# Recurrence of a hybrid encoder layer: the two score levels of a round are issued apart, the second behind the product with the turned inverse

## The chip, the cores and the metric

The kernel runs on one core of one Trainium2 chip. The metric is the device time of one execution in microseconds. TensorE is called PE here (with PEld for its weight loads), VectorE is DVE, ScalarE is ACT, SyncE is SP.

## What is computed

One step of a one-layer encoder trunk over 2048 prompt tokens and 8 short streams of 16 tokens: an adaptive norm, a projection, two parallel groups of recurrent heads (four HGRN2 heads of 128, eight RWKV-7 heads of 64), an output projection, then a two-level mixture of experts and a final norm. The change touches the recurrence alone. Its two parts are, in the reference:

```python
def step(S, blk):                       # HGRN2, by chunks of 64 tokens
    ...
    scores = jnp.einsum('bhtd,bhsd,bhtsd->bhts', qc, kc, decay)
    o = (jnp.einsum('bhts,bhsv->bhtv', scores, vc)
         + jnp.einsum('bhtd,bhdv->bhtv', qc * jnp.exp(b), S))
...
def step(S, inp):                       # RWKV-7, token by token
    sa = jnp.einsum('bhij,bhj->bhi', S, -kk_t)
    S = (S * jnp.exp(lw_t)[:, :, None, :] + sa[..., None] * (kk_t * a_t)[:, :, None, :]
         + v_t[..., None] * k_t[:, :, None, :])
    y = jnp.einsum('bhij,bhj->bhi', S, r_t)
```

## The kernel before

The program is a row of stages, one after the other: projections (to about 1,240 us), the recurrence (1,240 to about 1,930 us), the merge with the output projection, the experts. Each stage writes one instruction stream for each engine by hand. An engine works through its stream in the order written; `wait_ge` holds it until a counting semaphore has reached a value, and `then_inc` on an instruction raises one.

The recurrence (`recur`) takes 17 fronts of 128 tokens, each two chunks of 64. Step `i` of the loop handles the state-free work of front `f = i` and the state-bound work of the front before it (`b = i - 1`). One pass of this loop is called a step here, numbered by `f`: 0 has no back part, 1 to 15 are full, 16 (`TAIL`) holds the eight short streams and has four levels in place of six.

The state-free work has two parts that share PE:

- The inverse of a unit triangular 64 x 64 matrix for each of 8 heads and 2 chunks, built in doubling levels `lv`. A level is `make_y` (L1160, product of `LB` and `X` into `P_Y`), `turn_x` (L1168, the transpose of `X`, by a product with the identity, into `P_XT`) and `make_x` (L1180, the product with the turned inverse `XT`, added into `P_X`). Between them DVE masks `P_Y` into `Y` (`mask_y`, L1562, or L1560 at the first and last level), ACT copies `P_XT` to `XT` (`keep_xt`, L1417) and `P_X` to `X` (`keep_x`, L1411). So `make_x(lv)` waits for `mask_y(lv)` and `keep_xt(lv - 1)`, and `make_y(lv + 1)` waits for `keep_x(lv)`. The last level has `make_xt` (L1193) in place of `make_x`.
- The attention scores of the HGRN2 heads, for levels `n = 0` to 6: 8 products each (4 heads, 2 chunks, L1212) into one half of the bank `P_S`, even `n` left and odd `n` right. DVE writes them to `att` under the mask of the level (`mask_score`, L1573 and L1576, 128 x 256 elements each). `P_S` holds two levels, called a round `r = n // 2` in the code; the first level of a round waits until DVE has taken both of the round before (`scored`). DVE takes a round when `score_made` has been raised, once a round, with its last product.

Each full-precision product shows as two records in the trace, so 8 products are x16 and 16 products x32.

The order written on PE is, for levels 2 to 5: `make_y(lv)`, `turn_x(lv - 1)`, `score(lv - 1)`, `make_x(lv)`. The order on DVE, which the change leaves as it is:

```python
for lv in range(2, levels(f)):
    mask_y(f, lv)
    if back and lv == 2:
        y_centre(b)
    mask_score(f, lv - 1)
    if back and lv == 3:
        y_variance(b)
        y_bonus(b)
```

`y_centre`, `y_variance` (L1616, L1618) and `y_bonus` (L1625, L1627) are parts of the group norm of front `b`. ACT at level 2 has `keep_xt(1)`, then the square of the centred `y` (L1447, waits for `y_centre`), then `keep_x(2)`; at level 3 `keep_xt(2)`, `keep_x(3)`, then a logarithm and an exponential that wait for `y_variance`.

Of the kernel before, what the change touches and what calls it, by code (L numbers as in the profile page):

```python
# [43 lines left out]
HK_B, HK_KD, HK_Q, HK_K = [N_LEVELS + n for n in range(4)]  # L44
# [34 lines left out]
def sem_of(nc, names, name):  # L79

    names.append(nc.alloc_semaphore(name))
    return names[-1]
# [767 lines left out]
def recur(nc, t, bonus, ends):  # L850

    names = []
    with ExitStack() as ctx:
# [5 lines left out]
        def ev(name):  # L859

            if name not in sems:
                sems[name] = sem_of(nc, names, "re_" + name)
            return sems[name]
# [7 lines left out]
        hkf = [sb(f"hkf{p}", [128, 4, N_HK, 128]) for p in range(2)]  # L871
# [41 lines left out]
        P_X, P_Y, P_XT, P_S, P_ST, P_O = [ctx.enter_context(nc.psum_tensor(f"re_P{b}", [128, 512], F32)) for b in range(6)]  # L913
# [5 lines left out]
        def chunk(c):  # L919
            return slice(CH * c, CH * c + CH)  # L920
# [25 lines left out]
        def levels(f):  # L946
            return N_LEVELS if f < TAIL else DEC.bit_length() - 1
# [77 lines left out]
        def _(eng):  # L1025
# [145 lines left out]
            def make_x(f, lv):  # L1171

                for g in range(2):
                    eng.wait_ge(ev("y_kept"), before(f, 10) + 2 * (lv - 1) + g + 1)
                    if lv > 1:
                        eng.wait_ge(ev("xt_kept"), before(f, 8) + 2 * (lv - 2) + g + 1)
                    left, right = (XT0, Y1) if lv == 1 else (XT, Y)
                    for h in range(4 * g, 4 * g + 4):
                        for c in range(2):
                            ins = eng.matmul(P_X[chunk(c), 64 * h:64 * h + 64], left[chunk(c), h, :], right[chunk(c), h, :],  # L1180
                                             start=(lv == 1 and h == 0), stop=(h % 4 == 3), skip_group_check=True)
                ins.then_inc(ev("x_made"), 1)

            def make_xt(f):

                lv = levels(f) - 1
                left = Y5 if lv == 5 else Y3
                eng.wait_ge(ev("xt_kept"), before(f, 8) + 2 * (lv - 2) + 2)
                for g in range(2):
                    eng.wait_ge(ev("y_kept"), before(f, 10) + 2 * (lv - 1) + g + 1)  # L1190
                    for h in range(4 * g, 4 * g + 4):
                        for c in range(2):
                            ins = eng.matmul(P_XT[chunk(c), 64 * h:64 * h + 64], left[chunk(c), h, :], XT[chunk(c), h, :],  # L1193
                                             start=(h == 0), stop=(h % 4 == 3), skip_group_check=True)
                ins.then_inc(ev("xtf_made"), 1)


            def score(f, r):

                if 2 * r > levels(f):  # L1200
                    return
                p = f % 2
                if r == 0:
                    eng.wait_ge(ev("x0_kept"), f + 1)
                else:
                    eng.wait_ge(ev("scored"), before(f, 7) + 2 * r)
                for n in range(2 * r, min(2 * r + 2, levels(f) + 1)):
                    a, b = (HK_K, HK_Q) if n == 0 else (n - 1, n - 1)
                    for h in range(4):
                        o = 256 * (n % 2) + 64 * h  # L1210
                        for c in range(2):
                            ins = eng.matmul(P_S[chunk(c), o:o + 64], hkf[p][:, h, a, chunk(c)], hkf[p][:, h, b, chunk(c)],  # L1212
                                             start=(n % 2 == 0 and h == 0), stop=(h == 3), skip_group_check=True)
                ins.then_inc(ev("score_made"), 1)

            def turn_kd(f):

# [22 lines left out]
            for i in range(TAIL + 1):  # L1240
                f, b = i, i - 1
                p = f % 2
                back = b >= 0
                if back:
                    h_update(b)
                    h_inter(b, 0)
                    from_state(b, 0)
                    from_values(b, 0)
                eng.wait_ge(ev(f"front_in{p}"), 128 * (f // 2 + 1) + (64 if f == TAIL else 0))
                if f:  # L1250
                    eng.wait_ge(ev("x_kept"), before(f, 8))
                turn(f, RK_V, P_X)
                if f:
                    eng.wait_ge(ev("y_kept"), before(f, 10))
                turn(f, RK_B0, P_Y)
                if back:
                    solve(b, 0)
                    eng.wait_ge(ev("s_kept"), 2 * f)
                turn(f, RK_B1, P_XT)
                eng.wait_ge(ev("tok_kept"), 3 * f + 1)  # L1260
                products(f, RK_B0, (P_S, P_X))
                if back:
                    to_state(b, 0)
                    y_from_state(b, 0)
                eng.wait_ge(ev("tok_kept"), 3 * f + 3)
                products(f, RK_B1, (P_Y, P_XT))
                if back:
                    h_inter(b, 1)
                    h_intra(b)
                turn_x0(f)  # L1270
                if back:
                    from_state(b, 1)
                    from_values(b, 1)
                make_y(f, 1)
                if back:
                    solve(b, 1)
                make_x(f, 1)
                if back:
                    to_state(b, 1)
                    y_from_state(b, 1)  # L1280
                score(f, 0)
                if back:
                    y_out(b)
                for lv in range(2, levels(f)):
                    make_y(f, lv)
                    turn_x(f, lv - 1)
                    score(f, lv - 1)
                    if lv < levels(f) - 1:
                        make_x(f, lv)
                    else:  # L1290
                        make_xt(f)
                turn_kd(f)
                from_tokens(f)


            p = TAIL % 2
# [7 lines left out]
            for q in range(4):  # L1304
                if q >= 2:
                    eng.wait_ge(ev("std_begun"), q - 1)
                for m in range(4):
                    ins = eng.transpose((P_X, P_Y)[q % 2][:, 128 * m:128 * m + 128], srow[:, q, 128 * m:128 * m + 128], ident)
# [3 lines left out]
            for m in range(4):  # L1312
                ins = eng.transpose(P_XT[0:RW_N, 128 * m:128 * m + 128], ST[:, m, :], ident)
# [4 lines left out]
            for h in range(4):  # L1318
                o = slice(128 * h, 128 * h + 128)
                for c in range(2):  # L1320
                    eng.matmul(out_o(chunk(c), h), att[p][chunk(c), h, :], tmb[p][chunk(c), 0, o], start=(h == 0), stop=False, skip_group_check=True)
            for n in range(2):
                for h in range(4):
                    for g in range(4):
                        ins = eng.matmul(out_o(quarter(g), h), qbd[n][:, h, quarter(g)], Sd[:, 2 * g + n, h, :], start=False, stop=(n == 1 and h == 3),
                                         skip_group_check=True)
# [3 lines left out]
            for n in range(2):  # L1330
                for h in range(8):
                    for g in range(4):
                        ins = eng.matmul(out_g(quarter(g), h), ard[n][half(h), h // 2, 0, quarter(g)], STd[half(h), g, h // 2, n, :],
                                         start=False, stop=(n == 1 and h == 7), skip_group_check=True)
# [3 lines left out]
            for n in range(2):  # L1338
                for h in range(4):
                    o = slice(128 * h, 128 * h + 128)  # L1340
                    for g in range(4):
                        if n and h == 0:
                            eng.wait_ge(ev("sd_kept"), g + 1)
                        ins = eng.matmul(banks[g][:, o], kdT[p][quarter(g), o], hd[n][quarter(g), o], start=(h == 0), stop=(h == 3), skip_group_check=True)
                ins.then_inc(ev("upd_made"), 1)
                if n == 0:
                    eng.wait_ge(ev("g_kept"), 2 * TAIL + 1)
                    for h in range(8):
                        for c in range(2):
                            ins = eng.matmul(out_g(chunk(c), h), XTF[p][chunk(c), h, :], G[chunk(c), 64 * h:64 * h + 64],  # L1350
                                             start=False, stop=(h == 7), skip_group_check=True)
                    ins.then_inc(ev("sa_made"), 1)
            eng.wait_ge(ev("sad_kept"), 1)
            for n in range(2):
                for h in range(8):
                    for g in range(4):
                        ins = eng.matmul(out_y(quarter(g), h), ard[n][half(h), h // 2, 1, quarter(g)], STd[half(h), g, h // 2, n, :],
                                         start=False, stop=False, skip_group_check=True)
            ins.then_inc(ev("ys_made"), 1)
            eng.wait_ge(ev("ys_made"), 2 * TAIL + 1)  # L1360
            for h in range(8):
                for c in range(2):
                    ins = eng.matmul(out_y(chunk(c), h), LB[p][chunk(c), h, 1, :], SA[chunk(c), 64 * h:64 * h + 64],
                                     start=False, stop=(h == 7), skip_group_check=True)
            ins.then_inc(ev("yo_made"), 1)
            for g in range(4):
                eng.wait_ge(ev("sd_kept"), 5 + g)
                for kind, right in ((2, vd), (1, SAd)):
                    for n in range(2):
                        for h in range(8):  # L1370
                            o = slice(256 * n + 64 * (h // 2), 256 * n + 64 * (h // 2) + 64)
                            ins = eng.matmul(banks[g][half(h), o], tok[p][quarter(g), kind, 64 * h:64 * h + 64], right[n][quarter(g), 64 * h:64 * h + 64],
                                             start=(kind == 2 and n == 0 and h < 2), stop=(kind == 1 and n == 1 and h >= 6), skip_group_check=True)
                ins.then_inc(ev("std_made"), 1)
            for q in range(4):
                eng.wait_ge(ev("std_kept"), q + 1)
                for m in range(4):
                    ins = eng.transpose(banks[q][:, 128 * m:128 * m + 128], STd[:, q, m, :, :].rearrange("p s v -> p (s v)"), ident)
# [1163 lines left out]
```

## Time and profile before

| | |
|---|---|
| median of 3 runs | 3448.4 us (3444.95 to 3451.6) |
| the profiled execution: time, span | 3456.8 us, 3455.0 us |
| granted TensorE clock, mean of the span | 0.939 of full speed |
| PE busy over the span | 2997.6 us (87%) |
| DVE, ACT busy over the span | 1368.5 us (40%), 982.8 us (28%) |

The profiled execution is a single one, 8.4 us above the median of the runs. Times of single instructions are read from it; in the timeline the first column is the start in us from the span's start, the second the time from the first start to the last end of the merged rows, and the bracket is the idle time of that engine before it, with what ended it.

### The profile page before, as it was taken

The numbers are of one execution on the slowest core, as the hardware profiler recorded it, in microseconds if no ns is written. First come the engines' busy times: TensorE is split into PE (matmuls) and PEld (weight loads), VectorE is DVE, ScalarE is ACT, GpSimd is POOL, SyncE is SP. The second block draws the span as 40 slices with busy tenths as digits, with TensorE's granted clock in tenths as the row PEclk, the third lists the DMA queues.
The fourth block names the chain that finished last, engine by engine and source line by source line (L and its number), as shares of the span: only waits on it lengthen the run. The fifth ranks groups of instructions, "written<-read, shape, count | busy, mean of one in ns | idle before, by whom it ended". The sixth has DMA issues, their size and how long they took to land. (4 is left out here: it accounts for less than half of the span.)

```text
span 3455.0 us, 67244 instructions
## 1 busy us (share of the span) xinstructions
PE 2997.6 (87%) x28271; PEld 1796.4 (52%) x28272; DVE 1368.5 (40%) x3251; ACT 982.8 (28%) x1762; POOL 184.9 (5%) x281
## 2 busy tenths in 40 slices
PE   3899998998989659999999589958999999999930
PEld 1344444444444358888888445535555555555510
DVE  2410156455555535555555334452222112121246
ACT  2421244444434413323323111211222122222223
POOL 0000000000000000000000000000101001010024
PEclk7999999999999879999999799979999999999965
DMA  6233224122232295556553453355886568686746
GB/s 237 78 98 133 103 97 138 52 104 101 90 133 85 102 238 143 143 149 172 163 157 92 142 178 121 122 165 182 294 321 241 193 240 311 225 297 216 262 155 219
DMA packets 373004, 577.74 MB, mean 167 GB/s; under 512 B 31490, under 2 KB 199482, under 8 KB 369728
## 3 DMA queue, kind: packets, MB, share of 16 engines
q1 hardware_dynamic: 337632, 467.22, 40.4%
q0 software_dynamic: 18080, 72.10, 6.3%
q10 hardware_dynamic: 17088, 35.40, 3.3%
q8 instruction: 164, 2.69, 0.3%
q14 instruction: 40, 0.33, 0.0%
HBM read 429.04 MB, written 145.62 MB: 166 GB/s over the span
## 5 line engine op out<-in xcount | busy, mean ns | idle before, releaser
L2309 PE MATMUL moe_PG<-wgu,moe_xT 128*64 128x256 f32 x5248 | 582.1, 380 | 0.7 <-ACT moe_xT L2241 0.7
L441 PE MATMUL pj_P<-pj_hT,pj_wc 128*128 128x512 f32 x1280 | 561.0, 594 | 3.6 <-ACT pj_stage L559 3.6
L2309 PEld LDWEIGHTS moe_PG<-wgu,moe_xT 128*64 128x64 f32 x5248 | 377.3, 137 | 226.2 <-issue 47.5
L441 PEld LDWEIGHTS pj_P<-pj_hT,pj_wc 128*128 128x128 f32 x1280 | 240.9, 190 | 304.5 <-issue 304.5
L2316 PE MATMUL moe_PY<-wd,moe_hT 128*64 128x512 f32 x1312 | 317.7, 603 | 0.0
L1879 PE MATMUL merge_PO<-merge_w,merge_mT 128*128 128x512 f32 x544 | 243.9, 607 | 2.2 <-DMA merge_w<-in_w_out 2.2
L2244 ACT ACT_TABLE_LOAD x82 | 105.2, 1283 | 491.1 <-issue 491.0
L1879 PEld LDWEIGHTS merge_PO<-merge_w,merge_mT 128*128 128x128 f32 x544 | 104.4, 195 | 128.6 <-issue 128.6
L2224 DVE TENSOR_TENSOR moe_sg<-moe_sg,moe_PG 128x128 f32<-128x128 f32 x164 | 46.3, 282 | 290.8 <-ACT moe_sg L2244 290.8
L2228 DVE COPY moe_hT<-moe_PH 128x128 f32<-128x128 f32 x164 | 47.8, 291 | 273.1 <-PE moe_PH L2301 273.1
L2316 PEld LDWEIGHTS moe_PY<-wd,moe_hT 128*64 128x64 f32 x1312 | 81.9, 136 | 120.2 <-issue 86.8
L2231 DVE COPY moe_y<-moe_PY 128x512 f32<-128x512 f32 x82 | 56.7, 691 | 208.3 <-PE moe_PY L2316 208.3
L2263 POOL COPY moe_row<-moe_rows 128x1 int32 x83 | 15.2, 183 | 2126.1 <-issue 1336.9
L1160 PE MATMUL re_P<-re_X,re_LB 64*64 64x64 f32 x2656 | 96.7, 220 | 25.8 <-ACT re_X L1411 23.0
L362 PE MATMUL pj_P<-pj_wt,pj_hT 128*128 128x512 f32 x256 | 114.6, 601 | 1.2 <-ACT pj_hT L518 1.2
L473 PE MATMUL pj_P<-pj_wt,pj_hT 128*128 128x512 f32 x256 | 114.1, 599 | 0.0
L386 PE MATMUL pj_P<-pj_hT,pj_hk 128*128 128x512 f32 x256 | 111.4, 593 | 0.0
L1160 PEld LDWEIGHTS re_P<-re_X,re_LB 64*64 64x64 f32 x2656 | 85.4, 135 | 33.5 <-ACT re_X L1411 29.7
L1417 ACT COPY re_XT<-re_P 128x256 f32<-128x256 f32 x132 | 42.7, 375 | 168.7 <-PE re_P L1168 168.7
L2246 ACT ACTIVATE moe_sg<-moe_PG 128x128 f32<-128x128 f32 x82 | 22.8, 278 | 226.3 <-PE moe_PG L2309 226.3
L2266 POOL DMA_INDIRECT moe_xg<-scratch_h,moe_row x83 | 80.9, 975 | 67.2 <-POOL moe_row L2263 67.2
L791 DVE SCALAR_TENSOR_TENSOR pj_lf<-pj_P,pj_z 128x512 f32<-128x512 f32 (+1 forms) x20 | 12.2, 612 | 181.3 <-ACT pj_z L623 181.3
(373 smaller groups left out, 4222.8 us busy)
## 6 DMA issues: line engine op xcount, KB each, us to landing
wgu<-in_w_gate SPq DMA_DIRECT2D x32, 2048.0 KB, 9.3
wgu<-in_w_up SPq DMA_DIRECT2D x32, 2048.0 KB, 14.9
wd<-in_w_down SPq DMA_DIRECT2D x32, 2048.0 KB, 16.6
re_hkf<-scratch_hk SPq DMA_DIRECT2D x64, 640.0 KB, 8.3
scratch_hk<-pj_hk SPq DMA_DIRECT2D x16, 1536.0 KB, 5.6
re_rkf<-scratch_rk SPq DMA_DIRECT2D x68, 320.0 KB, 4.9
scratch_y_rows<-moe_y ACTq DMA_DIRECT2D x164, 128.0 KB, 5.0
scratch_rk<-pj_rk SPq DMA_DIRECT2D x16, 1280.0 KB, 4.8
```

What stands on the lines that cost most here:

```text
L362: ins = eng.matmul(P[2 + m % 2][:, :], rows[:, k, :], wt[:, k, :], start=(k == 0), stop=(k == KD - 1))
L386: ins = eng.matmul(out, lora_w[:, k, c0:c0 + 128], rhs, start=(s == 0 and k == 0), stop=(s == 1 and k == KD - 1))
L441: ins = eng.matmul(bank[:, :], wc[:, j, k, :], hT[:, k, token(g) + 1:token(g) + 513], start=(k == 0), stop=(k == KD - 1))
L473: ins = eng.matmul(PQ[:, :], rows[:, k, :], wt[:, k, :], start=(k == 0), stop=(k == KD - 1))
L1160: ins = eng.matmul(P_Y[chunk(c), 64 * h:64 * h + 64], LB[f % 2][chunk(c), h, 0, :], X[chunk(c), h, :], start=(h == 0), stop=(h % 4 == 3), ...
L1879: ins = eng.matmul(PO[:, half, :], mT[:, n % 2, k, :], w[:, k, 512 * half:512 * half + 512], start=(k == 0), stop=(k == KD - 1))
L2228: eng.tensor_copy(hT[:, j, :], PH[:, j, 0:128]).then_inc(ev("hT_kept"), 1)
L2231: eng.tensor_copy(y[:, :], PY[:, :]).then_inc(ev("y_kept"), 1)
L2244: eng.activation(sg[:, 0, :], PG[:, 0, 0:128], ACT.Sigmoid).then_inc(ev("sigmoid_made"), 1)
L2266: eng.indirect_dma_start(xg[:, :], None, t["h2"].rearrange("t (h c) -> (t h) c", h=2), bass.IndirectOffsetOnAxis(ap=row[:, 0:1], axis=0)). ...
L2309: ins = eng.matmul(PG[64 * c:64 * c + 64, j, 0:256].rearrange("p (a b) -> p a b", a=2), x_rows, wgu[p][:, :, k, o:o + 128], start=(k == 0) ...
L2316: ins = eng.matmul(PY[64 * n:64 * n + 64, :], hT[:, j, 64 * c:64 * c + 64], wd[p][:, 2 * c + j, 512 * n:512 * n + 512], start=(j == 0 and ...
```

## The change

`score(f, n)` now issues one level `n` in place of a round of two. Before the level loop both levels of round 0 are issued together, as before. In the loop the even level `2 * lv - 2` stays where the pair was, and the odd level `2 * lv - 1` comes behind `make_x(lv)`; at the last level, where `make_xt` is, both stay ahead of it. The wait for `scored` stays with the even level and `score_made` is raised with the odd one (or with the last level there is), so the counts do not change, and DVE and ACT are not touched. With six levels the calls that issue something are 2 and 3 at `lv = 2`, 4 and 5 at `lv = 3`, and 6 alone at `lv = 4`. With four levels (step 16) they are 2 and 3, and 4 alone.

```diff
-            def score(f, r):
-
-                if 2 * r > levels(f):
+            def score(f, n):
+
+                if n > levels(f):
                     return
-                p = f % 2
-                if r == 0:
+                p, r = f % 2, n // 2
+                if n == 0:
                     eng.wait_ge(ev("x0_kept"), f + 1)
-                else:
+                elif n % 2 == 0:
                     eng.wait_ge(ev("scored"), before(f, 7) + 2 * r)
-                for n in range(2 * r, min(2 * r + 2, levels(f) + 1)):
-                    a, b = (HK_K, HK_Q) if n == 0 else (n - 1, n - 1)
-                    for h in range(4):
...
+                a, b = (HK_K, HK_Q) if n == 0 else (n - 1, n - 1)
+                for h in range(4):
...
-                ins.then_inc(ev("score_made"), 1)
+                if n % 2 or n == levels(f):
+                    ins.then_inc(ev("score_made"), 1)
...
                 score(f, 0)
+                score(f, 1)
...
                     turn_x(f, lv - 1)
-                    score(f, lv - 1)
+                    score(f, 2 * lv - 2)
                     if lv < levels(f) - 1:
                         make_x(f, lv)
+                        score(f, 2 * lv - 1)
                     else:
+                        score(f, 2 * lv - 1)
                         make_xt(f)
```

## Rows read from the trace of the kernel before

**Rows 1.** The page: span and number of instructions.
```profile
span 3455.0 us, 67244 instructions
```

**Rows 2.** Busy time by engine, 590 us of the recurrence: length, then PE, PEld, DVE, ACT, POOL.
```profile
1270.00:1860.00 590.00, 547.98 (x14528) 508.53 (x14528) 337.43 (x773) 181.73 (x459) 0.00 (x0) 0.99 0.55 154
```

**Rows 3.** Waits, 1270 to 1860 us: total us, times, longest us.
```profile
ACT re_X L1411 <- PE re_P L1180: 48.6, 50, 2.3
...
DVE re_Y L1562 <- PE re_P L1160: 24.9, 16, 2.6
...
PE re_P L1160 <- ACT re_X L1411: 20.6, 44, 0.5
```

**Rows 4.** Timeline, step 9, level 2 and the start of level 3.
```profile
1612.96 1.01 PEld L1212 LDWEIGHTS re_P<-re_hkf 128*64 128x64 f32 x32
...
1614.04 1.01 PEld L1180 LDWEIGHTS re_P<-re_Y,re_XT 64*64 64x64 f32 x32
...
1614.64 0.63 ACT L1447 ACTIVATE re_ysq<-re_yc 128x512 f32<-128x512 f32 x1 [0.91 <-DVE re_yc L1611]
1615.24 0.65 ACT L1411 COPY re_X<-re_P 128x256 f32<-128x256 f32 x2
1615.66 1.01 PEld L1160 LDWEIGHTS re_P<-re_X,re_LB 64*64 64x64 f32 x32 [0.61 <-ACT re_X L1411]
```

**Rows 5.** Timeline, step 9, level 3 and the start of level 4.
```profile
1616.59 1.02 PEld L1168 LDWEIGHTS re_P<-re_const,re_X 64*64 64x64 f32 x32
...
1616.86 0.76 DVE L1562 TENSOR_TENSOR re_Y<-re_P,re_const 128x256 f32<-128x256 f32 x2 [1.43 <-PE re_P L1160]
1617.67 1.01 PEld L1212 LDWEIGHTS re_P<-re_hkf 128*64 128x64 f32 x32
...
1617.79 0.65 ACT L1417 COPY re_XT<-re_P 128x256 f32<-128x256 f32 x2 [1.91 <-PE re_P L1168]
1618.76 1.01 PEld L1180 LDWEIGHTS re_P<-re_Y,re_XT 64*64 64x64 f32 x32
...
1618.88 0.92 DVE L1576 COPY_PREDICATED re_att<-re_const,re_P 128x256 f32<-128x256 uint32 x2 [1.26 <-PE re_P L1212]
...
1619.95 0.65 ACT L1411 COPY re_X<-re_P 128x256 f32<-128x256 f32 x2 [1.51 <-PE re_P L1180]
1620.38 1.01 PEld L1160 LDWEIGHTS re_P<-re_X,re_LB 64*64 64x64 f32 x32 [0.61 <-ACT re_X L1411]
```

**Rows 6.** Timeline, step 9, level 4.
```profile
1621.20 0.69 DVE L1627 TENSOR_TENSOR re_vb<-re_vb,re_rows 128x512 f32<-128x512 f32 x1
...
1621.81 0.75 DVE L1562 TENSOR_TENSOR re_Y<-re_P,re_const 128x256 f32<-128x256 f32 x2
1622.39 0.55 PEld L1212 LDWEIGHTS re_P<-re_hkf 128*64 128x64 f32 x16
...
1623.00 1.03 PEld L1180 LDWEIGHTS re_P<-re_Y,re_XT 64*64 64x64 f32 x32
...
1623.12 0.45 DVE L1576 COPY_PREDICATED re_att<-re_const,re_P 128x256 f32<-128x256 uint32 x1 [0.57 <-PE re_P L1212]
```

**Rows 7.** Timeline, step 9, earlier: first mask of `Y1`, then the first `make_x`.
```profile
1606.24 0.78 DVE L1560 COPY_PREDICATED re_Y<-re_const,re_P 128x256 f32<-128x256 uint32 x2 [1.27 <-PE re_P L1160]
...
1606.75 0.19 PEld L1180 LDWEIGHTS re_P<-re_Y,re_XT 64*64 64x64 f32 x2
```

**Rows 8.** Timeline, ACT at level 2 of step 1, and the row of all these squares.
```profile
1297.68 0.63 ACT L1447 ACTIVATE re_ysq<-re_yc 128x512 f32<-128x512 f32 x1 [0.91 <-DVE re_yc L1611]
1298.28 0.65 ACT L1411 COPY re_X<-re_P 128x256 f32<-128x256 f32 x2
...
L1447 ACT ACTIVATE re_ysq<-re_yc x15: 630/630/644, 1297.7 to 1852.4; 128x512 f32<-128x512 f32 x15
```

**Rows 9.** Timeline, level 2 of step 10: `turn_x` resumed, then ACT.
```profile
1653.17 0.56 PE L1168 MATMUL re_P<-re_const,re_X 64*64 64x64 f32 x12 [1.42 <-issue]
...
1654.30 0.64 ACT L1447 ACTIVATE re_ysq<-re_yc 128x512 f32<-128x512 f32 x1
...
1655.94 0.65 ACT L1411 COPY re_X<-re_P 128x256 f32<-128x256 f32 x2 [0.99 <-PE re_P L1180]
```

**Rows 10.** Timeline, two copies of 588 ns back to back on ACT.
```profile
1596.49 1.07 ACT L1405 COPY re_tok<-re_P 128x512 f32<-128x512 f32 x2 [0.46 <-PE re_P L1128]
```

**Rows 11.** Timeline, step 0 (no back part), level 4, DVE.
```profile
1261.66 0.76 DVE L1562 TENSOR_TENSOR re_Y<-re_P,re_const 128x256 f32<-128x256 f32 x2 [1.77 <-PE re_P L1160]
```

**Rows 12.** Timeline, the same instruction of steps 8 and 9.
```profile
1581.89 0.17 DVE L1618 TENSOR_SCALAR re_rst<-re_rst 128x8 f32<-128x8 f32 x1
...
1620.40 0.17 DVE L1618 TENSOR_SCALAR re_rst<-re_rst 128x8 f32<-128x8 f32 x1
```

More of the change, by code:

```diff
@@ L1195, in make_xt @@
                 ins.then_inc(ev("xtf_made"), 1)
-            def score(f, r):
-                if 2 * r > levels(f):
+            def score(f, n):
+                if n > levels(f):
                     return
-                p = f % 2
-                if r == 0:
+                p, r = f % 2, n // 2
+                if n == 0:
                     eng.wait_ge(ev("x0_kept"), f + 1)
-                else:
+                elif n % 2 == 0:
                     eng.wait_ge(ev("scored"), before(f, 7) + 2 * r)
-                for n in range(2 * r, min(2 * r + 2, levels(f) + 1)):
-                    a, b = (HK_K, HK_Q) if n == 0 else (n - 1, n - 1)
-                    for h in range(4):
[L1210 to L1213, printed above, removed]
-                ins.then_inc(ev("score_made"), 1)
+                a, b = (HK_K, HK_Q) if n == 0 else (n - 1, n - 1)
+                for h in range(4):
+                    o = 256 * (n % 2) + 64 * h
+                    for c in range(2):
+                        ins = eng.matmul(P_S[chunk(c), o:o + 64], hkf[p][:, h, a, chunk(c)], hkf[p][:, h, b, chunk(c)],
+                                         start=(n % 2 == 0 and h == 0), stop=(h == 3), skip_group_check=True)
+                if n % 2 or n == levels(f):
+                    ins.then_inc(ev("score_made"), 1)
             def turn_kd(f):
```

## Prediction

> **What bounds the kernel now.** I read the page first: the span is 3455.0 us [rows 1]. The stages follow each other, so a change in the recurrence is worth what it moves there. The windows view says that PE is busy 548 of 590 us of that stage at a granted clock of 0.99, DVE 337 and ACT 182 [rows 2]. PE sets the pace; the question is what it stands idle for. The view of waits answers: 44 times it waited about 0.5 us, 20.6 us in all, for the copy of `X` that `make_y` needs [rows 3]. That is the hole into which the change puts work. The same view holds a warning: DVE waited for `make_y` before L1562 only 16 times, where 15 full steps have three such masks each [rows 3]. Part of the missing ones are at level 2, where DVE comes from other work; the rest are at level 4, and there the timeline has to be read.
>
> In the timeline of step 9, level 3, see first the hole: `make_x(3)` at 1618.76, its copy at 1619.95, `make_y(4)` at 1620.38, so 1.62 us from product to product, while `make_x` takes PE only 1.08 or 1.09 [rows 5]. See then DVE: it takes both score levels at 1618.88, as soon as they are there, and is busy without a gap through the norm's `y_variance` and `y_bonus` until `mask_y(4)` at 1621.81, which starts in the tail of L1627 (1621.20 + 0.69) and not on PE's word [rows 5, 6]. On PE's word it would have begun 1.20 us behind `make_y(4)`, as at level 3 (1616.86 against 1615.66), that is at 1621.58 [rows 5]. So at level 4 DVE already runs 0.23 us late, unseen, because PE reaches `make_x(4)` only at 1623.00 [rows 6].
>
> **PE's own times.** A group of x32 is followed by the next after 0.93 us if both are of one shape of tile (1615.66 to 1616.59) and after 1.08 if a score group (128*64) meets a 64*64 one (1616.59 to 1617.67) [rows 4, 5]; so a switch costs 0.15. A score group of x16 takes 0.61 to the next (1622.39 to 1623.00), which is 0.93 / 2 + 0.15 [rows 6]. Splitting a pair gives two switches more, one on each side of the group that is moved. No products are added, and no DMA is issued or waited for at another place; the loads that SP issues hang on `kd_made` at the end of a step and move with it.
>
> The Trainium skill, TensorEngine Tiling (Array Packing), Key Properties, states that changing the tiling mode drains the engine, which speaks against splitting. The trace has 0.15 us for it [rows 4, 5]. The skill's TensorE: Matmul & The Clock Gate, Single matmul latency, puts a drain at about 175 ns; by that the lateness worked out below would grow by 2 x 0.025 = 0.05 us a step, some 0.8 us in all. Without any drain it would shrink by 0.07.
>
> **Level 3, PE's side.** `score(4)` stays at 1617.67. `make_x(3)` follows after 0.61, at 1618.28 instead of 1618.76. Its turned inverse is there: ACT starts the copy at 1617.79 and a half takes 0.375, so 1618.2, and the second half is wanted 0.5 later [rows 5]. `score(5)` follows after 1.09 at 1619.37. `make_y(4)` could start at 1619.98 by PE, and at 1618.28 + 1.62 = 1619.90 by the copy; so 1619.98, which is 0.40 earlier than 1620.38. Unhindered, that is the gain of a moved level: a hole of 0.61 filled by 0.47 of products and a switch.
>
> **Level 3, DVE's side.** `score_made` now comes with level 5, behind `make_x(3)`. From the start of a group of 8 products to DVE's reading of it are 0.73 us (1622.39 to 1623.12) [rows 6]. So `mask_score(2)` starts at 1619.37 + 0.73 = 1620.10 instead of 1618.88: 1.22 later. Queued behind it on DVE are `y_variance`, `y_bonus` and `mask_y(4)`, 2.93 us of back-to-back work (1618.88 to 1621.81) [rows 5, 6], none of which can pass. `mask_y(4)` therefore starts at 1623.03. PE gets its first half some 0.48 later: the mask of L1560 at 1606.24 released `make_x` at 1606.75, 0.51 with an operation of 440 ns, and this one has 415 [rows 7]. `make_x(4)` starts at 1623.51 instead of 1623.00: **0.51 us later**, though PE is ready for it at 1622.60. The 0.40 gained ahead of `make_y(4)` is swallowed by this new wait of about 0.9, and 0.51 is lost besides. From there on all PE work follows from `make_x(4)`, so nothing of it is recovered. ACT is no second hindrance: its logarithm and exponential come 1.22 later and end near 1622.3, when `turn_x(3)` is just ready, 1.2 ahead of need. The wait of `score(6)` for `scored` is met at 1621.0. 15 steps x 0.51 = **+7.6 us**.
>
> **Level 2.** The odd level moves the same way, but DVE has `y_centre` ahead of `mask_score(1)` and then a slack before `mask_y(3)` [rows 4, 5], so it is not late: it would read at 1615.1, end at 1616.0, and is wanted at 1616.8. Here ACT is the limit. `make_x(2)` at 1613.57 instead of 1614.04 [rows 4] would be copied at 1614.8, but ACT must first square the centred `y`, from 1614.64 for 0.63, and this start does not move. Two copies of 588 ns start 0.48 to 0.49 apart [rows 10], so ACT can take the next some 0.10 before the end of the first: 1615.17 instead of 1615.24. The gain is 0.07, not 0.40. This holds where the copy starts 0.60 behind the square, as in step 1 [rows 8]: 8 of the 15 steps. Where PE had stalled in or ahead of `turn_x`, the square was early (step 10: 1654.30 against 1655.94) and the full 0.40 is there [rows 9]: 5 steps. Two lie between (gaps of 0.68 and 0.79: 0.15 and 0.26). The sum is 8 x 0.07 + 5 x 0.40 + 0.41 = **-3.0 us**.
>
> **Steps 0 and 16.** Step 0 has no norm on DVE, and L1562 waits for PE at level 4 too [rows 11]: both moves gain 0.40, -0.8. Step 16 moves one level at level 2, behind the same square: -0.1.
>
> **Sum.** 7.6 - 3.0 - 0.9 = **+3.7 us**, of the profiled execution 3456.8 to 3460.5, of the median 3448.4 to 3452.1. What the trace of before does not show is the price of a switch in the new places and ACT's hand-over from the square. Ends: with no switch price at all the lateness is 0.43 and with 0.40 gained in every level 2 the sum is 6.5 - 6.0 - 0.9 = -0.4; with the lateness at 0.60 (a switch 0.045 dearer, as it enters twice) and nothing gained at level 2 of full steps it is 9.0 - 0.9 = +8.1. I take the value between from the rows nearest in place. Differences within 0.2%, 6.9 us, are about what a measurement of this kernel cannot tell from no change; the sum lies inside.
>
> **Rivals.**
> - *The hole is filled and nothing is late.* All 32 moves of steps 0 to 15 gain 0.40 and step 16 too: about -13 us, 3435. For it: DVE is busy only 337 of 590 us [rows 2]. Against: the back-to-back chain into `mask_y(4)` has only 1623.00 - 1621.81 - 0.48 = 0.71 us of slack, and 1.22 is asked of it [rows 6].
> - *The lateness is larger.* This is the side of a measurable loss. If a score group between two 64*64 groups costs a switch of 0.25 and not 0.15, `mask_score(2)` is later by 0.20 more, and the loss is 15 x 0.71 - 3.0 - 0.7 = +7.0 us: 3455.4. From there it decides. For it: each level now has four switches where it had two, and no row shows a score group straight behind `make_x`. Against: both kinds of neighbours in [rows 5, 6] give the same price.
> - *It comes out at nothing.* PE now has a wait of 0.9 in each step; it also has stalls of its own, marked as issue, such as 1.42 us in step 10 [rows 9]. If those that fall near the new wait are hidden by it, and level 2 gains more than the clean steps promise, +3.7 shrinks to within 1 us of zero: 3448.
>
> **How the numbers follow.** My forecast 0.60, the larger lateness 0.22, nothing 0.10, the filled hole 0.08. The forecast is 3452. The filled hole's 3435 and a larger loss than 3459 are left out, together less than 2 in 10, so the range is 3445 to 3459; it takes in the two ends above (3448.0 and 3456.5) and some 3 us of scatter, as the runs of before show. Faster by over 0.2% is the filled hole, 0.08. Slower is most of the larger lateness and the part of the forecast that scatter lifts over the bound: 0.20 + 0.06 = 0.26. Within 0.2% is the rest, 0.66.
>
> **What the profile after would show.** `mask_score(2)` starts 1.8 us behind `make_x(3)` where it was 0.12. `make_x(4)` has a new idle time of about 0.9 us on PE, released by DVE's L1562, 15 times, and the view of waits has it at some 13 us. PE's waits for the copy of `X` fall from 44 by the 15 at level 3, and those at level 2 shrink from 0.47 to about 0.3. The distance between the same instruction of steps 8 and 9, 38.51 us without a stall between them [rows 12], grows by 0.51 - 0.07 = 0.44 to 38.95. I am wrong if `mask_y(4)` begins before 1.20 us after `make_y(4)` plus 0.5; if ACT takes `keep_x(2)` without delay; or if a score group of x16 takes other than 0.61 to its successor.

## The result, and the profile after

The changed kernel took 3460.8 us (median of 7 runs, 3452.9 to 3464.0) against 3448.4 for the kernel before in the same session (7 runs, 3445.0 to 3452.8): a ratio of 1.0031, 95% interval 1.0019 to 1.0043. It is slower, by 6.6 to 14.8 us; forecast were +3.7 us and a range to 3459. In a second session (below) the ratio was 1.0020, 1.0011 to 1.0029. The two together speak for some 7 to 9 us.

The page of the changed kernel begins with:

```profile
span 3459.9 us, 67244 instructions
```

The windows view over the same 590 us of the recurrence [rows 2] has PE busy as long as before, with 235 matmul records fewer (14293 against 14528). At the mean of 24.6 records a us that is 9.5 us of work. It is a rough figure: the window cuts the steps of the two executions at different places, and a few matmul records are missing from a trace.

```profile
1270.00:1860.00 590.00, 548.95 (x14293) 507.48 (x14294) 330.74 (x757) 176.92 (x450) 0.00 (x0) 0.99 0.55 154
```

The view of waits of the changed kernel for that stretch (total us, times, longest us) answers to [rows 3]:

```profile
PE re_P L1180 <- DVE re_Y L1565: 10.5, 14, 0.8
PE re_P L1160 <- ACT re_X L1414: 7.7, 19, 0.5
PE re_P L1168 <- issue: 7.7, 6, 3.1
```

PE's wait for the copy of `X` fell from 20.6 us in 44 to 7.7 in 19, as the change meant. A wait for `mask_y(4)` took its place, 10.5 us in 14, where there was none; some 13 us had been forecast. Eleven of the 14 are of 0.83 us. The other three, of steps 4, 7 and 10, are of 0.61, 0.23 and 0.46, because PE had already been late in the products ahead of them.

The timeline of step 12 of the changed kernel, which had no stall, shows levels 2 to 4. (DVE's and ACT's lines lie three higher than before: L1565 is `mask_y`, L1579 `mask_score`, L1630 the end of `y_bonus`, L1450 the square, L1414 `keep_x`; L1211 is the score product.) Level 2, against [rows 4]:

```profile
1738.62 0.55 PEld L1211 LDWEIGHTS re_P<-re_hkf 128*64 128x64 f32 x16
...
1739.24 1.03 PEld L1180 LDWEIGHTS re_P<-re_Y,re_XT 64*64 64x64 f32 x32
...
1740.31 0.63 ACT L1450 ACTIVATE re_ysq<-re_yc 128x512 f32<-128x512 f32 x1 [0.92 <-DVE re_yc L1614]
1740.34 0.55 PEld L1211 LDWEIGHTS re_P<-re_hkf 128*64 128x64 f32 x16
...
1740.84 0.63 ACT L1414 COPY re_X<-re_P 128x256 f32<-128x256 f32 x2
...
1741.25 1.01 PEld L1160 LDWEIGHTS re_P<-re_X,re_LB 64*64 64x64 f32 x32 [0.36 <-ACT re_X L1414]
```

The square starts when it always did and holds up the copy: 0.53 from the one to the other, where it was 0.60. From the first score product to `make_y(3)` are 2.63 us against 2.70. The gain is 0.07, as worked out.

Levels 3 and 4, against [rows 5, 6]:

```profile
1743.26 0.55 PEld L1211 LDWEIGHTS re_P<-re_hkf 128*64 128x64 f32 x16
...
1743.88 1.03 PEld L1180 LDWEIGHTS re_P<-re_Y,re_XT 64*64 64x64 f32 x32
...
1744.97 0.55 PEld L1211 LDWEIGHTS re_P<-re_hkf 128*64 128x64 f32 x16
...
1745.59 1.01 PEld L1160 LDWEIGHTS re_P<-re_X,re_LB 64*64 64x64 f32 x32
...
1745.71 0.92 DVE L1579 COPY_PREDICATED re_att<-re_const,re_P 128x256 f32<-128x256 uint32 x2 [2.50 <-PE re_P L1211]
...
1748.03 0.69 DVE L1630 TENSOR_TENSOR re_vb<-re_vb,re_rows 128x512 f32<-128x512 f32 x1
1748.64 0.75 DVE L1565 TENSOR_TENSOR re_Y<-re_P,re_const 128x256 f32<-128x256 f32 x2
1749.11 1.01 PEld L1180 LDWEIGHTS re_P<-re_Y,re_XT 64*64 64x64 f32 x32 [0.97 <-DVE re_Y L1565]
```

See how the hole ahead of `make_y(4)` has gone: no bracket at 1745.59, and 2.33 us from the first score product against 2.71. Then follow DVE: idle for 2.50 us, it begins `mask_score(2)` only at 1745.71, 1.83 behind `make_x(3)` where it was 0.12, and reaches `mask_y(4)` 2.93 later. PE's weight loads wait 0.97 for it (the bracket) and its products 0.83. From `make_y(3)` to `make_x(4)` are 7.86 us against 7.34, a loss of 0.52 (forecast 0.51).

The kdT copy closes each step. Between those of steps 11 and 12 lie 38.96 us:

```profile
1716.37 0.59 ACT L1459 COPY re_kdT<-re_P 128x512 f32<-128x512 f32 x1 [1.82 <-PE re_P L1220]
...
1755.33 0.59 ACT L1459 COPY re_kdT<-re_P 128x512 f32<-128x512 f32 x1 [1.83 <-PE re_P L1220]
```

The forecast was 38.95, from 38.51 [rows 12]. So a clean step was foretold to a hundredth, and the whole was not. The 15 full steps took 594.05 us before and 600.87 after, in the timeline from the first kdT copy to the last but one: +6.8, where the forecast had 7.6 - 3.0 = +4.6. In both kernels that is 15 clean steps and 16.4 or 16.5 us more, which I call the excess. It is in the steps in which PE stood idle for no releaser that the profile shows (issue). What these stalls are, and what they do to a gain, was left open by the prediction, and is what the experiments had to find besides its mechanism.

### The profile page after: what moved, and what is told of

Read it like the earlier page. It is cut to its first block and busy times, and to the rows that moved or that the text cites. A ratio compares the mean times of both kernels' runs of the same rounds, so it can differ in the third digit from the quotient of the medians.

```text
span 3459.9 us, 67244 instructions
## 1 busy us (share of the span) xinstructions
PE 3005.9 (87%) x28271; PEld 1802.7 (52%) x28272; DVE 1369.4 (40%) x3251; ACT 981.0 (28%) x1762; POOL 184.0 (5%) x281
## 3 DMA queue, kind: packets, MB, share of 16 engines
q8 instruction: 164, 2.69, 0.3%
## 5 line engine op out<-in xcount | busy, mean ns | idle before, releaser
L1180 PE MATMUL re_P<-re_Y,re_XT 64*64 64x64 f32 x2112 | 80.4, 222 | 14.6 <-DVE re_Y L1565 11.3
```

## The experiments

All ratios are to runs of the kernel before on the same chip in the same session (median 3451.5, 3451.9 and 3453.1 in the three sessions). The recurrence has no other way to be seen apart from the rest than its trace: "full steps" is the time from the kdT copy of step 0 to that of step 15, "excess" what this has over 15 times its clean step. Both are of one execution each, the profiled one.

### One move at a time, the norm's operations out of the way, and the change again

Only the condition of the move changes in the first two, `lv == 2` or `lv == 3`:

```diff
-                    if lv < levels(f) - 1:
+                    if lv != 2 and lv < levels(f) - 1:
+                        score(f, 2 * lv - 1)
+                        make_x(f, lv)
+                    elif lv < levels(f) - 1:
                         make_x(f, lv)
                         score(f, 2 * lv - 1)
```

> The odd score level is moved at level 2 alone; at level 3 the pair stays ahead of make_x. Forecast theory (DVE late at level 4 is the loss): nothing is lost at level 4, a clean step lasts 38.52 - 0.07 = 38.45 us, the whole is 0.5 (step 0, 16) + 15 x 0.07 to 0.2 = 1.5 to 3.5 us faster than before, ratio 0.9990 to 0.9996. Rival (splitting a pair costs by itself, through two more switches of tile shape and PE's stalls marked issue): slower than before, by about half of the loss of the change, +3 to +6 us.

> The odd score level is moved at level 3 alone. Forecast theory: the whole loss is here, a clean step lasts 38.52 + 0.51 = 39.03 us, the whole is 15 x 0.51 - 0.4 = +7.2 us, ratio 1.0021. Rival (splitting costs by itself): about the same as with the move at level 2 alone, +3 to +6 us, and the two together make the change.

Measured: level 2 alone 3448.9 us, ratio 1.0000 (0.9988 to 1.0012); level 3 alone 3460.2 us, 1.0026 (1.0014 to 1.0038). The clean steps were 38.43 and 39.03 us, against 38.45 and 39.03 expected. The loss is all at level 3. Splitting a pair does not cost by itself, though it adds two switches of tile shape at level 2 too. The gain expected at level 2, 1.5 to 3.5 us, lies inside the interval and is not shown by the runs, only by the step. (The profiled execution of level 2 alone had full steps of 587.2 us, 6.8 less than before, with an excess of only 10.8; level 3 alone had 602.2 and 16.8. So the excess moves by some us from trace to trace, and a term of 2 us can't be read from one pair of them.)

The third takes `y_bonus` out of DVE's chain into `mask_y(4)`:

```diff
                     if back and lv == 3:
                         y_variance(b)
+                    if back and lv == min(4, levels(f) - 1):
                         y_bonus(b)
```

> The changed kernel with y_bonus (two DVE operations, 0.68 and 0.69 us) taken behind mask_y(4) and mask_score(3) in steps 1 to 15, everything else as changed. Forecast theory: the chain into mask_y(4) is 1.37 us shorter, so mask_y(4) starts near its data and make_x(4) where PE is ready, 0.40 earlier than before the change: clean step 38.52 - 0.07 - 0.40 = 38.05, the whole 15 x 0.47 + 0.9 + 2.0 = 8 to 10 us faster than before, ratio 0.9971 to 0.9977. Rival (splitting costs by itself): slower than before still, ratio over 1.001.

Measured: 3445.3 us, 0.9986 (0.9976 to 0.9996); clean step 38.11. To go from slower to faster by moving two DVE operations of 0.68 and 0.69 us is what the mechanism says and what a price of the split could not do. The timeline of this kernel, step 12 (1700.3 to 1738.4 us), at level 4:

```profile
1729.59 0.92 DVE L1579 COPY_PREDICATED re_att<-re_const,re_P 128x256 f32<-128x256 uint32 x2 [2.50 <-PE re_P L1211]
...
1730.40 1.02 PEld L1168 LDWEIGHTS re_P<-re_const,re_X 64*64 64x64 f32 x32
...
1731.20 0.75 DVE L1565 TENSOR_TENSOR re_Y<-re_P,re_const 128x256 f32<-128x256 f32 x2
...
1731.68 0.63 ACT L1420 COPY re_XT<-re_P 128x256 f32<-128x256 f32 x2
...
1732.15 1.04 PEld L1180 LDWEIGHTS re_P<-re_Y,re_XT 64*64 64x64 f32 x32
```

`mask_y(4)` is no longer last: 0.95 us from it to `make_x(4)`, without idle time. The clean step is 0.06 over the 38.05 I had expected because ACT's exponential, behind the later `y_variance`, now holds the copy of `P_XT` up a little (it starts 1.28 behind `turn_x` of 1730.40, where 1.20 is the rule [rows 5]). The whole gained 4.8 us by the ratio (interval 1.4 to 8.3) and 6.2 between the medians, not the 8 to 10 expected. 15 clean steps, each 0.41 shorter, promise 6.1 us, which agrees; what did not come is the 2.0 us that the expectation had again counted for level 2 in stalled steps.

The fourth is the changed kernel once more.

> The changed kernel again, beside the same runs of before as the others. Forecast theory: the difference of two executions of the recurrence is 15 x 0.44 - 1 = 5 to 7 us and what more was measured (1.0031, interval 1.0019 to 1.0043) is scatter, so the ratio comes out at 1.0015 to 1.0025. Rival (the change adds stalls of PE marked issue, or moves later stages): the ratio is again 1.003, and the profile shows more stall time in the recurrence than the 15 us of the profile shown.

Measured: 3458.5 us (3453.1 to 3462.0), 1.0020 (1.0011 to 1.0029). Full steps 601.58, excess 17.5. So 1.0031 was in part scatter, and my +3.7 us (1.0011) is at the lower edge of this interval too.

### The stalls: fewer loads

PE's unexplained waits of the kernel before lie in the first 25 us of a step, such as 1.42 us in step 10 [rows 9]. Step 13 of the kernel before begins at 1748.1 us. The DMA view from 1750 to 1768 us has the 16 engines full (share of 16 engines last):

```profile
q1 hardware_dynamic: 9372, 5.26, 106.0%
q8 instruction: 3, 0.05, 1.1%
```

q1 are the kernel's loads, 5.26 MB of them, and q8 the packets that bring instructions. On the whole page of before q8 has 164 packets with 2.69 MB, so 16 KB each. The loads of a front, most of them `hkf` (4 x 640 KB), go out together at the end of a step. To test that the instruction packets wait behind them, `hkf` was left unloaded in steps 2 to 15 (a load of 64 bytes into an unused tile stands in; the scores and the state of the HGRN2 heads are then made from other fronts' data):

```diff
-                    if f < TAIL:
+                    if 2 <= f < TAIL:
+                        eng.dma_start(spare[4 * f - 8 + c:4 * f - 7 + c, :], hk3[c:c + 1, c, 0, k:k + 16]).then_inc(ev(f"front_in{p}"), 16)
+                    elif f < TAIL:
                         eng.dma_start(hkf[p][:, c, :, :], hk3[:, c, :, k:k + 128]).then_inc(ev(f"front_in{p}"), 16)
```

> The kernel before, with the loads of hkf (4 x 640 KB) of steps 2 to 15 replaced by loads of 64 bytes into an unused tile, so that the scores are made of the data of steps 0 and 1; all instructions of PE, DVE and ACT stay. Theory of the stalls (PE's waits marked issue in the first 25 us of a step come from its instruction packets standing behind the front's loads in the DMA queues): the 16.4 us by which steps 1 to 15 exceed 15 clean steps of 38.52 fall to under 6, the whole is 9 to 14 us faster than before. Rival (the stalls are tied to positions in the instruction stream, whatever the DMAs do): they stay, 0 to 2 us faster.

> The changed kernel with the same small loads. Theory of the stalls: every full step is near its clean length of 38.96, so the changed kernel is slower than the kernel before with small loads by 15 x 0.44 - 0.9 = 5.7 us, and the excess is under 6 us again. Rival (the change adds stalls of its own, at the extra switches of tile shape): the difference is 8 us or more and the excess stays above 12.

Measured: before with small loads 3445.4 us, 0.9980 (0.9970 to 0.9990); after with small loads 3454.0 us, 1.0006 (0.9997 to 1.0016). The excess fell from 16.4 to 2.2 us and from 16.5 to 2.6. The row of the kdT copies (first and last start) gives the same for both, before and after with small loads:

```profile
L1459 ACT COPY re_kdT<-re_P x17: 585/585/586, 1274.1 to 1883.7; 128x512 f32<-128x512 f32 x17
```

```profile
L1462 ACT COPY re_kdT<-re_P x17: 585/585/585, 1270.1 to 1887.2; 128x512 f32<-128x512 f32 x17
```

609.6 and 617.1 us for steps 1 to 16. Without the loads nearly all of the stalls are gone. The place in the instruction stream has a part too: with all loads, the kernel before has a marked stall at L1168, some 24 us into the step, in steps 4, 7, 10 and 13 and in no other (2.51, 1.15, 1.42 and 0.83 us), and the changed kernel's repetition has one there in the same four (1.41, 1.15, 1.42, 1.10). So the rival named something real, but not a cause that is enough: with small loads none of these is left.

Without them the change costs the full steps 587.05 - 580.02 = 7.0 us (15 x 0.44 = 6.6 and 0.4 of excess); the two medians differ by 8.6 us, with intervals of some 3 us each. That is over the 8 us of the rival, but its other sign, an excess above 12, did not come.

The whole was expected to be 9 to 14 us faster than the kernel before and came out 6.5 faster, though its full steps were 14.0 us shorter. The rest is not in the recurrence. From the last kdT copy to the end of the span are 1567.2 us with small loads and 1556.6 before. The pages, that of before first, show one copy of a row of token numbers more in the experts, 84 for 83. The one thing changed there is the data, so it seems that the experts' routing came out otherwise:

```profile
L2263 POOL COPY moe_row<-moe_rows 128x1 int32 x83 | 15.2, 183 | 2126.1 <-issue 1336.9
```

```profile
L2266 POOL COPY moe_row<-moe_rows 128x1 int32 x84 | 15.3, 182 | 2118.6 <-issue 1319.6
```

In the view of waits, such a copy waits 9.6 us for PE in the mean (789.3 us in 82 before, 799.0 in 83 with small loads), so one more costs about that. All three kernels with small loads have 83 of these waits, all the others 82. The whole times of small-load kernels can be compared with each other, and not with those of the rest.

These two traces also show what a stall can do to a gain, in step 0, where both moves gain and which still stalls once, at level 5. Before with small loads (L1163 is `make_y`, L1171 `turn_x` here; the first row is level 1, the second level 5):

```profile
1247.74 1.15 PE L1163 MATMUL re_P<-re_X,re_LB 64*64 64x64 f32 x32 [0.69 <-ACT re_X L1436]
...
1265.27 1.15 PE L1163 MATMUL re_P<-re_X,re_LB 64*64 64x64 f32 x32 [0.46 <-ACT re_X L1414]
...
1268.48 1.87 PE L1171 MATMUL re_P<-re_const,re_X 64*64 64x64 f32 x31 [2.01 <-issue]
...
1274.14 0.58 ACT L1459 COPY re_kdT<-re_P 128x512 f32<-128x512 f32 x1 [3.10 <-PE re_P L1223]
```

After with small loads:

```profile
1243.76 1.15 PE L1163 MATMUL re_P<-re_X,re_LB 64*64 64x64 f32 x32 [0.69 <-ACT re_X L1439]
...
1256.34 1.50 PE L1163 MATMUL re_P<-re_X,re_LB 64*64 64x64 f32 x32
...
1260.94 1.15 PE L1163 MATMUL re_P<-re_X,re_LB 64*64 64x64 f32 x32 [0.46 <-ACT re_X L1417]
...
1264.36 1.97 PE L1171 MATMUL re_P<-re_const,re_X 64*64 64x64 f32 x31 [2.23 <-issue]
...
1270.12 0.58 ACT L1462 COPY re_kdT<-re_P 128x512 f32<-128x512 f32 x1 [3.10 <-PE re_P L1223]
```

From `make_y(1)` to `make_y(5)` the change is ahead by 17.53 - 17.18 = 0.35 us, with part of its gain already lost in a group that took 1.50 instead of 1.15. The stall is then longer (2.23 against 2.01) and the groups behind it slower, and at the kdT copy 26.40 stand against 26.36: of the 0.8 us forecast for step 0, 0.04 is left in this pair. It looks as if PE had got to missing instructions earlier and waited for them longer. One pair is not much: with bunched or spread loads, step 0 lasts from 25.8 to 29.9 us between the same two points in the eleven traces, which hides 0.8 us.

In the full steps the same is seen many times over. Step 10 of the kernel before, from the scores of level 2 to those of level 3:

```profile
1653.66 1.15 PE L1212 MATMUL re_P<-re_hkf 128*64 128x64 f32 x32
...
1656.37 1.15 PE L1160 MATMUL re_P<-re_X,re_LB 64*64 64x64 f32 x32 [0.47 <-ACT re_X L1411]
...
1658.38 1.15 PE L1212 MATMUL re_P<-re_hkf 128*64 128x64 f32 x32
```

Step 10 of the changed kernel:

```profile
1659.05 0.69 PE L1211 MATMUL re_P<-re_hkf 128*64 128x64 f32 x16
...
1661.37 1.15 PE L1160 MATMUL re_P<-re_X,re_LB 64*64 64x64 f32 x32
...
1663.48 0.57 PE L1168 MATMUL re_P<-re_const,re_X 64*64 64x64 f32 x13 [0.39 <-issue]
...
1663.98 0.69 PE L1211 MATMUL re_P<-re_hkf 128*64 128x64 f32 x16
```

To `make_y(3)` are 2.32 us against 2.71: the gain of the move is there. From `make_y(3)` to the scores of level 3 are 2.61 against 2.01: PE stalls once more and loses it. The second stretch lasts 2.01 in all 15 full steps of the kernel before. In the changed kernel, its repetition and the three others that move the level at level 2 with bunched loads (level 2 alone, `y_bonus` later, both later), it lasts 2.25 to 2.88 in each of the steps 7, 10 and 13. That is 0.24 to 0.87 us lost, 0.49 in the mean of the 15, where level 2 had 0.37 to give.

### Both hindrances away, with and without the split

In the next two ACT's square also goes behind `keep_x(2)`:

```diff
                     keep_xt(f, lv - 1)
+                    if lv < levels(f) - 1:
+                        keep_x(f, lv)
                     if back and lv == 2:
                         eng.wait_ge(ev("y_centred"), b + 1)
                         eng.activation(ysq[:, :], yc[:, :], ACT.Square).then_inc(ev("y_squared"), 1)
-                    if lv < levels(f) - 1:
-                        keep_x(f, lv)
```

> The changed kernel with y_bonus behind mask_y(4) on DVE, as in the earlier run, and on ACT the square of the centred y behind keep_x(2) in place of ahead of it. Theory (ACT's square was the limit at level 2): the clean step goes from 38.11 to 38.11 - 0.33 = 37.78; the whole is 4 to 9 us faster than with y_bonus alone if the stalls do not take it back, ratio to before 0.996 to 0.998. Rival (PE's supply of instructions gives the pace once the holes are filled): the clean step falls so, but the excess of the stalled steps grows by as much, ratio 0.998 to 0.999 as with y_bonus alone.

> The kernel before with the same two moves on DVE and ACT and the scores as before. Theory (in the kernel before both have slack: mask_y(4) 0.71 us, the square 0): clean step 38.52, nothing changes, ratio 0.9995 to 1.0005, so the gain of the other runs needs the split of the scores. Rival (y_bonus and the square alone were in the way): faster by 0.1% or more.

Measured: with the split 3443.3 us, 0.9978 (0.9969 to 0.9988), clean step 37.83; without it 3456.1 us, 1.0009 (0.9998 to 1.0020), clean step 38.53. The clean step fell from 38.11 by 0.28 (expected 0.33), so the square was the limit at level 2, and without the split both moves are worth nothing. The 15 clean steps promise 10.4 us and the runs give 7.6 with an interval of 4.1 to 10.7. The rival had the excess grow by as much as the clean steps fell; it was 15.0 us, against 16.4 before, so it did not grow.

> The changed kernel with y_bonus and the square later, and with the small loads of hkf. Theory: 15 clean steps of 37.83 and little excess, so the recurrence is 15 x 0.69 + 0.8 = 11 us shorter than that of the kernel before with small loads (644.7 us in the trace), 633 to 635 us; the whole 3434 to 3436. Rival (a part of the gain is lost elsewhere than in the stalls): 637 us or more.

Measured: 3436.6 us, 0.9948 (0.9933 to 0.9963), clean step 37.83. From the first product of the recurrence to the last kdT copy it took 637.1 us in the trace, where 633 to 635 were expected; step 8 was 3.4 us over its clean length, and the excess was 4.9 where the two other kernels with small loads had 2.2 and 2.6. That much is on the rival's side, and one execution does not tell a stray stall from a rule. The medians of this kernel and of before with small loads differ by 8.8 us over two sessions.

### Loads spread over the step

If bunched loads make the stalls, spreading the same bytes must do what leaving them out did. SP issues `rkf` at the end of a step as before, and each part of `hkf` behind one copy of `X` in the step after:

```diff
+            def load_scores(f):
...
                 for c in range(4):
+                    if f >= 2:
+                        eng.wait_ge(ev("x_kept"), before(f - 1, 8) + 2 * c + 1)
                     if f < TAIL:
                         eng.dma_start(hkf[p][:, c, :, :], hk3[:, c, :, k:k + 128]).then_inc(ev(f"front_in{p}"), 16)
...
                     if b + 2 <= TAIL:
                         load_back(b + 2)
+                if i + 2 <= TAIL:
+                    load_scores(i + 2)
```

> The kernel before with all its loads, but the four hkf loads of a front (640 KB each) issued one by one, each behind one copy of X of the next step, instead of all at the end of a step. Theory of the stalls: the instruction packets no longer stand behind 2.6 MB of loads, the excess of steps 1 to 15 over 15 x 38.52 falls from 14 to 16 us to under 8, the whole is 5 to 12 us faster. Rival (the amount of loads, not their order, makes the stalls): excess 12 us or more, ratio 0.999 to 1.001.

> The changed kernel with the loads spread in the same way. Theory: slower than the kernel before with spread loads by 15 x 0.44 less 0.1 to 0.9 for steps 0 and 16, that is 5.7 to 6.6 us, clean step 38.96. Rival (the split adds stalls): 9 us or more.

> The candidate: scores split, y_bonus and the square later, loads spread. Theory: clean step 37.83, excess under 8, 14 to 20 us faster than the kernel before, ratio 0.9942 to 0.9960. Rival (one of the gains excludes the other): no better than 0.997.

Measured: before with spread loads 3442.3 us, 0.9961 (0.9948 to 0.9974), excess 6.5; the change with spread loads 3450.0 us, 0.9988 (0.9978 to 0.9998), clean step 38.95, excess 6.9; all together 3435.1 us, 0.9940 (0.9924 to 0.9956), clean step 37.83, excess 7.9. The DMA view of the first of them, from 1750 to 1768 us, where the kernel before had moved 5.26 MB:

```profile
q1 hardware_dynamic: 2991, 2.25, 41.2%
q8 instruction: 4, 0.07, 1.6%
```

This window lies 7 us into step 13 (from 1742.8), where that of the kernel before lay 2 us into it. In the same part of the step (1744.7 to 1762.7) q1 moved 3.45 MB, 63.3%. In both kernels the DMA engines are full from some 2 us into the step. In the kernel before they stay so until some 22 us into it, and its marked stalls lie 15 to 25 us into a step; with spread loads they stay so until some 12 us and have only short bursts after that.

With the stalls mostly gone the change costs 7.7 us between the medians and 591.17 - 584.34 = 6.8 in the full steps, near 15 x 0.44 again and under the rival's 9. The last kernel is 18 us faster than the kernel before between the medians (20.7 by the ratio), the best of all.

## Why the prediction was wrong

- **The mechanism held.** The hole ahead of `make_y(4)` was filled (0.38 of 0.40), `mask_score(2)` was read 1.83 behind `make_x(3)`, nothing on DVE passed it, `make_x(4)` came 0.52 later (0.51), and the clean step grew by 0.44 to 0.45 (0.44). One move at a time gave its two parts, 38.43 and 39.03, and moving `y_bonus` turned the sign. The wait on PE came out at 0.83 in a clean step, 14 times in the window, and so at 10.5 us and not 13.
- **A switch of tile shape costs 0.15.** Spacings of 0.62 and 1.09 to 1.10 were met in the new places; the dearer switch, the rival of a larger lateness, is out.
- **Level 2 in clean steps: 0.07,** as the overlap on ACT said.
- **The step that failed is that of level 2 in the stalled steps.** The prediction put it so: "Where PE had stalled in or ahead of `turn_x`, the square was early ... and the full 0.40 is there: 5 steps." The square was early there and the gain came: 2.33 and 2.32 us in steps 7 and 10 of the changed kernel where there had been 2.70. What the prediction put at nothing is what PE does next: it stalled once more at level 3 and lost 0.28 and 0.60 there, with nothing lost at that place in the kernel before. Over steps 7, 10 and 13 of the five kernels with the move at level 2 and bunched loads, the mean loss there was 0.49. In step 13 it ran short already at level 2 (3.55 us). In the two others of the five, 2 and 4, this execution had no early square, and the gain was the 0.07 of a clean step. With small gains in two more steps I had counted -3.0 us for level 2; 15 x 0.07 = -1.0 is what clean steps give, and the 2.0 us on top of it were not kept.
- **The -0.8 of step 0 may have failed in the same way.** In the pair with small loads 0.04 of it was left; the other traces scatter too much to say. Without the 2.0 us of level 2 the forecast would have been +5.7, and without both terms +6.5. The full steps of the four pairs of traces give 6.8 to 7.5, near 7.6 - 1.0 = 6.6 and above the 4.6 of the forecast; each pair is two executions and scatters.
- **The third rival had the stalls the wrong way round.** I let a new wait hide later stalls. The stalls of the kernel before lie ahead of it in the step, and it is the gains ahead of a stall that are swallowed, while the loss at level 4, behind it, stays whole: from `make_y(4)` to the kdT copy are 9.75 us in every full step of the changed kernel, 8.86 before. In steps 4, 7 and 10 a stall did end inside the new wait (0.61, 0.23, 0.46 in place of 0.83), but it had not been there before, so nothing was saved.
- **The rest of the miss is scatter, as far as is known.** The kernel before had a median of 3448.4 in the scored session as in the forecast, so the base was not at fault there. The changed kernel was 12.4 us above it between the medians, 10.7 by the ratio; in the next session, with 11 and 34 runs, 7.0 both ways, which +6.5 fits. My range went to 3459 on a count of one kernel's scatter of 3 us, while the kernel before alone ranged over 3442 to 3462 in 34 runs. With the failed terms put right the forecast would have been 3448.4 + 6.5 = 3454.9, and 3460.8 is still 5.9 above that; so it took the failed step and this scatter together to leave the range.
- **What stays open.** That the instruction packets stand behind the data packets in the DMA queues is inferred: loads left out or spread take most of the stalls away, but no row shows a packet waiting. Why stalls come back at the same place of steps 4, 7, 10 and 13 was not tried either. Which bounds the stalls in step 0, where loads of the first fronts are under way, was not tried.

## What to carry to other kernels

When work is moved into a hole of one engine, follow the semaphore of the moved work to its reader and list what is queued behind the reader: here 0.40 us gained on PE cost 1.22 on a DVE that had 0.71 of slack, though DVE was idle 43% of the time. Before a gain is counted in a step that holds a wait marked issue, ask whether the gain lies ahead of it: here the time gained ahead of such stalls was lost again behind them (0.37 gained, 0.49 lost), while the time lost behind them stayed lost. And if stalls of that kind stand in the shadow of bunched loads, spread the loads: that alone was worth 0.4% here, more than the whole question of where to put the scores.

## What the runs showed of the hardware that was not expected

PE's stalls marked issue hang on DMA traffic. With the 16 engines full (106% in the view) through 18 us of a step, the 15 full steps had an excess of 14.3 to 17.5 us in six of the eight traces with all loads bunched (10.8 and 12.5 in the other two); with 2.6 MB a step less it was 2.2, 2.6 and 4.9, and with the same bytes spread 6.5 to 7.9. The Trainium skill, Runtime: NRT & Kernel Launch, Instruction fetch mechanics, says that each engine's instructions are refilled in blocks of 16 KiB and that the cost of crossing a block is mostly hidden. The packet size agrees (2.69 MB in 164 packets). The hiding does not hold here, if these stalls are what they are inferred to be: spreading the loads made the kernel about 0.4% faster, and the measurement decides.

A stall also has a shape that no bracket marks. In step 13 of the changed kernel, behind a marked stall of 1.65 us, a group of 32 that takes 1.15 took 1.95 and one of 16 that takes 0.69 took 1.12:

```profile
1779.83 0.68 PE L1168 MATMUL re_P<-re_const,re_X 64*64 64x64 f32 x15 [1.65 <-issue]
...
1781.06 1.95 PE L1180 MATMUL re_P<-re_Y,re_XT 64*64 64x64 f32 x32
...
1782.93 1.12 PE L1211 MATMUL re_P<-re_hkf 128*64 128x64 f32 x16
```

So the sum of the marked waits is less than what the stalls cost: in that step the marked ones are 2.4 us and the excess is 4.0.
